# The RWKV scan of a two-block kernel: halves of heads interleaved, last tokens moved into the recurrence, chunk matrices from 32-row blocks

## What is computed

```python
def step(S, inp):
    r_t, w_t, k_t, v_t, kk_t, a_t = inp
    sa = jnp.einsum('bhvk,bhk->bhv', S, kk_t)
    S = (S * w_t[:, :, None, :]
         - sa[..., None] * (kk_t * a_t)[:, :, None, :]
         + v_t[..., None] * k_t[:, :, None, :])
    return S, jnp.einsum('bhvk,bhk->bhv', S, r_t)
```

## Time and profile before

| | us |
|---|---|
| median of 3 runs (lowest, highest) | 1706.77 (1698.46, 1707.61) |
| the profiled execution | 1702.17 |
| its span, first to last instruction | 1700.4 |
| first transpose to last addition of the scan | 567.3 to 755.2 |

### The profile page before, as it was taken

How to read it: one execution, slowest core, us unless ns; L and a number is a source line. 1 busy time by engine, 2 the same in 40 slices (tenths; PEclk the granted TensorE clock), 3 DMA queues, 4 the chain that set the end, 5 groups by cost and what they waited for, 6 DMA issues and landing times.

```text
span 1700.4 us, 32005 instructions
## 1 busy us (share of the span) xinstructions
PE 1561.2 (92%) x11384; PEld 1421.2 (84%) x11384; DVE 1072.5 (63%) x1815; ACT 838.1 (49%) x1443; POOL 411.8 (24%) x183
## 2 busy tenths in 40 slices
PE   5989879999699877778999999999999999999998
PEld 5975569999589756658899999999999988888886
DVE  3355356555666666746555989779999754555444
ACT  3445545555474311115445565667667554554554
POOL 1220102222024313001222423422221223222231
PEclk9986899999899998958999999999999999999999
DMA  6550125555134200003553555554344466566664
GB/s 225 184 161 0 50 75 185 185 185 184 64 124 149 88 1 1 2 1 124 163 164 134 187 173 183 181 158 137 130 148 138 137 195 196 186 197 190 195 194 149
DMA packets 66244, 234.80 MB, mean 138 GB/s; under 512 B 8216, under 2 KB 9256, under 8 KB 66176
## 3 DMA queue, kind: packets, MB, share of 16 engines
q1 hardware_dynamic: 65776, 232.31, 42.6%
q0 software_dynamic: 400, 1.59, 0.3%
HBM read 232.81 MB, written 1.06 MB: 138 GB/s over the span
## 4 chain that ended last, share of the span: by engine, by line
PE 72%; issue 15%; DVE 8%; ACT 2%; POOL 2%; DMA 0%; SPq 0%; POOLq 0%; DVEq 0%; ACTq 0%
PE psum L669 37%; PE psum L1154 20%; PE psum L968 4%; PE psum L683 4%; PE psum L1120 3%; DVE big L1391 2%; POOL w_lo L503 2%; PE psum L1092 1%; DVE w_lo L503 1%; PE psum L657 1%; DVE big L1503 1%; DVE big L1493 1%; DVE big L1515 0%; PE psum L1020 0%; PE psum L1017 0%
## 5 line engine op out<-in xcount | busy, mean ns | idle before, releaser
L669 PE MATMUL psum<-x_hi,w_hi 128*128 128x256 f32 (+1 forms) x2192 | 630.2, 287 | 34.8 <-DVE x_lo L1209 16.5
L503 POOL TENSOR_TENSOR w_lo<-ring,w_hi 128x1024 fp32r<-128x1024 f32 x144 | 358.0, 2486 | 1144.7 <-ACT w_hi L489 1144.7
L669 PE MATMUL psum<-x_lo,w_hi 128*128 128x256 f32 (+1 forms) x2192 | 624.8, 285 | 0.0
L669 PE MATMUL psum<-x_hi,w_lo 128*128 128x256 f32 (+1 forms) x2192 | 624.4, 285 | 0.0
L489 ACT ACTIVATE w_hi<-ring 128x1024 fp32r<-128x1024 f32 x434 | 455.9, 1051 | 111.2 <-PE psum L669 70.9
L669 PEld LDWEIGHTS psum<-x_hi,w_hi 128*128 128x128 f32 x2192 | 421.3, 192 | 42.0 <-issue 29.4
L503 DVE TENSOR_TENSOR w_lo<-ring,w_hi 128x1024 fp32r<-128x1024 f32 x290 | 364.4, 1257 | 138.0 <-ACT w_hi L489 137.2
L669 PEld LDWEIGHTS psum<-x_hi,w_lo 128*128 128x128 f32 x2192 | 421.7, 192 | 0.0
L669 PEld LDWEIGHTS psum<-x_lo,w_hi 128*128 128x128 f32 x2192 | 419.1, 191 | 0.1
L1771 DVE TENSOR_TENSOR h_lo<-big,h_hi 128x256 fp32r<-128x256 f32 x128 | 71.7, 560 | 152.9 <-ACT h_hi L2126 152.9
L1154 PE MATMUL psum<-w_hi,h_lo 128*128 128x512 f32 x512 | 157.7, 389 | 0.0
(11 more groups left out here) (293 smaller groups left out, 1773.5 us busy)
## 6 DMA issues: line engine op xcount, KB each, us to landing
ring<-experts SPq DMA_DIRECT2D x256, 512.0 KB, 3.5
ring<-w_ffn SPq DMA_DIRECT2D x66, 512.0 KB, 3.5
ring<-w_in SPq DMA_DIRECT2D x46, 512.0 KB, 3.7
ring<-w_mid SPq DMA_DIRECT2D x24, 512.0 KB, 3.5
ring<-w_out SPq DMA_DIRECT2D x16, 512.0 KB, 4.1
ring<-w_q SPq DMA_DIRECT2D x16, 512.0 KB, 4.3
ring<-w_cmp SPq DMA_DIRECT2D x8, 512.0 KB, 3.5
big<-bias_rows POOLq DMA_DIRECT2D x1, 1536.0 KB, 9.0
```

The costliest lines, as they stand in the source:

```text
L503: eng.tensor_tensor(w_lo[:, n % RING, :], ring[:, n % RING, :], w_hi[:, n % RING, :].bitcast(F32), ALU.subtract).then_inc(low_ready2 if n ...
L669: mm = pe.matmul(dst, w[:, slot, k * P:(k + 1) * P], x[:, k, t0:t0 + width], start=(n == 0), stop=(n == 3 * len(chunks) - 1))
```

## The change

- **Units.** The halves of a token group have their own `gram`, `ycol`, PSUM banks and semaphores, and run step by step in turn. `gram` has 7 slots a half instead of 10 (L4, L4T, L8T take those of L, LT, MT).
- **Last 16 tokens.** Their transposes, Grams, products and additions stand between the steps of the second group's recurrence, on PE and DVE; effects, one step and the addition remain behind it. The second group's transposes stand between the steps of the first recurrence, two a step.
- **Chunk matrices.** ACT writes kappa and beta of the turned group twice, masked by the parity of the chunk (`halves`). `carries` multiplies blocks of 32 tokens (two chunks) as 32x64 by 32x128 and 32x64 by 32x64, 80 matmuls a half, each block of rows into a bank of its own. The spreads over chunks on POOL and DVE are gone. ACT copies g after DVE's addition to f.
- **Conv pairs.** 16 pairs among the gate tiles instead of 8, the others at new places in the scan; 62 in all as before.
- The state has 3 slots instead of 9, and ACT's wait on `stay_ready` is gone.

`apply_power`, `second_products`, `third_product` and `effects` are the old matmuls with a half as argument, as are `add_power`, `add_effects` and `add_out` on DVE.

```diff
+    ("halves", 2), ("rowmask", 2), ("iota", P),
...
-tm = room(4, 4 * P)
+tm = room(2, 4 * P)
 scratch0 = at[0]
-gram = room(10, 4, P)
-ycol = room(4, P)
-f_t = room(4, 8, HD)
-g_c = room(4, 8, HD)
-state = room(4, 9, HD)
+gram = [room(7, 4, P) for _ in range(2)]
+ycol = [room(4, P) for _ in range(2)]
+f_t = room(4, 8 * HD)
+g_c = room(4, 8 * HD)
+state = room(4, 3, HD)
 top1 = at[0]
 stay = tm[:, 0, 0:14]
-
-
-expand0 = carve(8 * (T2 + 1), 2, 2, 8, HD)
-expand_g = carve(scratch0, 4, 2, 8, HD)
-expand = ((expand0[:, 0], expand0[:, 1], expand_g[:, 0]),
-          (expand_g[:, 3], expand_g[:, 2], expand_g[:, 1]))
-G_L, G_LT, G_MT, G_L2, G_L2T, G_L4, G_L4T, G_L8T, G_QT, G_RT = range(10)
+tm_kappa = carve(8 * (T2 + 1), 8, 2, HD)
+tm_beta = carve(8 * (T2 + 1) + 8 * P, 8, 2, HD)
+G_L, G_LT, G_MT, G_L2, G_L2T, G_QT, G_RT = range(7)
+G_L4, G_L4T, G_L8T = G_L, G_LT, G_MT
+FULL = {"turn": 4, "lt": (0, 4), "l": (2, 6), "qr": (0, 2), "mv": (6, 1), "l2": (4, 7), "l2t": (5, 0), "app0": (2, 3),
+        "l4": (4, 7), "l4t": (5, 0), "app1": (6, 1), "l8t": (2, 3), "app2": (4, 5), "app3": (6, 7),
+        "e": (0, 2), "o": (1, 3), "fg": (4, 0)}
+LAST = {"turn": 6, "lt": (3, 5), "l": (3, 5), "qr": (3, 5), "mv": (7, 3), "l2": (7, 3), "l2t": (7, 3), "app0": (4, 5),
+        "l4": (7, 3), "l4t": (7, 3), "app1": (6, 5), "l8t": (4, 7), "app2": (6, 5), "app3": (4, 3),
+        "e": (6, 5), "o": (7, 4)}
+banks = lambda tg: FULL if tg < 2 else LAST
+by_pair = lambda v: v.rearrange("p (r n) -> p r n", r=4)
+group = lambda tg: (tg * P, min(P, T2 - tg * P))
...
-        for hh in range(2):
-            for p in range(2):
-                u = 2 * tg + hh
-                if p == 0:
-                    pool.wait_ge(tm_ready, 4 * (tg + 1))
-                    if u > 0:
-                        pool.wait_ge(fg_sum, 2 * u - 1)
-                else:
-                    pool.wait_ge(app_ready, 4 * (u + 1))
-                for k, src in ((0, 3), (1, 1))[:2 - p]:
-                    a = (4 * hh + 2 * p) * HD
-                    pool.tensor_tensor(expand[p][k], tm[:, src, a:a + P].rearrange("p (h k) -> p h k", h=2).unsqueeze(2).to_broadcast([P, 2, 8, HD]),
-                                       const("chunk").unsqueeze(1).unsqueeze(3).to_broadcast([P, 2, 8, HD]),
-                                       ALU.mult).then_inc(spread_b, 1)
...
+    def grams(tg, hh, name, odd):
+        t0, nt = group(tg)
+        kinds = {"lt": ((beta, alpha), (kappa, alpha)), "l": ((alpha, beta),), "qr": ((beta, rho), (kappa, rho))}[name]
+        for k, (x, y) in enumerate(kinds):
+            for h in (odd, odd + 2):
+                c = gram_column(tg, name) + (2 * k + h // 2) * nt
+                mm = pe.matmul(psum[0:nt, banks(tg)[name][hh] + odd, c:c + nt], fm(x, 4 * hh + h, t0, nt),
+                               fm(y, 4 * hh + h, t0, nt), start=True, stop=True)
+        return mm
+    def product(tg, hh, name, a, rhs):
+        nt = group(tg)[1]
+        for h in range(4):
+            r = rhs(h)
+            c = column(tg, name) + h * P
+            mm = pe.matmul(psum[0:nt, banks(tg)[name][hh], c:c + r.shape[1]], gram[hh][0:nt, a, h, 0:nt], r,
+                           start=True, stop=True)
+        return mm
+    def first_products(tg, hh):
+        nt = group(tg)[1]
+        product(tg, hh, "mv", G_MT, lambda h: tm[0:nt, 1, (4 * hh + h) * HD:(4 * hh + h + 1) * HD]).then_inc(pow_sum[hh], 1)
+        product(tg, hh, "l2", G_LT, lambda h: gram[hh][0:nt, G_L, h, 0:nt]).then_inc(pow_sum[hh], 1)
+        product(tg, hh, "l2t", G_L, lambda h: gram[hh][0:nt, G_LT, h, 0:nt]).then_inc(pow_sum[hh], 1)
...
+    def carries(tg, hh):
+        b0 = FULL["fg"][hh]
+        for p in range(2):
+            for kind in range(5):
+                for x in range(2):
+                    h = 2 * p + x
+                    head = 4 * hh + h
+                    q = slice(x * HD, (x + 1) * HD)
+                    for r in range(4):
+                        rows = slice(32 * r, 32 * r + 32)
+                        c = p * P
+                        if kind == 0:
+                            mm = pe.matmul(psum[q, b0 + r, c:c + P], ycol[hh][rows, h, 0:HD],
+                                           tm_beta[rows, head].rearrange("p s k -> p (s k)"), start=True, stop=True)
+                        else:
+                            s = (kind - 1) // 2
+                            c += 2 * P + s * HD
+                            if kind % 2:
+                                mm = pe.matmul(psum[q, b0 + r, c:c + HD], tm_kappa[rows, head, s],
+                                               tm[rows, 1, head * HD:(head + 1) * HD], start=True, stop=False)
+                            else:
+                                mm = pe.matmul(psum[q, b0 + r, c:c + HD], tm_beta[rows, head, s],
+                                               ycol[hh][rows, h, HD:P], start=False, stop=True)
+        mm.then_inc(fg_sum[hh], 1)
+    def recur(tg, c):
+        n = 8 * tg + c
+        pe.wait_ge(state_ready, n + 1)
+        if tg < 2:
+            for h in range(8):
+                q = slice(h % 2 * HD, (h % 2 + 1) * HD)
+                mm = pe.matmul(psum[q, c % 2, h // 2 * HD:(h // 2 + 1) * HD], f_t[q, h // 2, c * HD:(c + 1) * HD],
+                               state[q, h // 2, n % 3, :], start=True, stop=True)
+            mm.then_inc(rec_sum, 1)
+        for h in range(8):
+            q = slice(h % 2 * HD, (h % 2 + 1) * HD)
+            mm = pe.matmul(psum[q, 2, h // 2 * P + c * CH:h // 2 * P + (c + 1) * CH], state[q, h // 2, n % 3, :],
+                           e_t[q, h // 2, c * CH:(c + 1) * CH], start=True, stop=True)
+        return mm
+    turn_in(0, range(16))
+    for tg in range(2):
         if tg > 0:
             pe.wait_ge(o_ready, tg)
         for hh in range(2):
+            if hh == 1:
+                pe.wait_ge(tm_ready, 6 * tg + 6)
             pe.wait_ge(kappa_ready, 2)
+            for name in ("lt", "l"):
                 for odd in range(2):
+                    grams(tg, hh, name, odd).then_inc(gram_sum[hh], 1)
+        for hh in range(2):
+            pe.wait_ge(gram_ready[0], 6 * tg + 2 + 2 * hh)
+            for odd in range(2):
+                grams(tg, hh, "qr", odd).then_inc(gram_sum[hh], 1)
+        pe.wait_ge(gram_ready[0], 6 * tg + 4)
+        pe.wait_ge(gram_ready[1], 6 * tg + 4)
+        first_products(tg, 0)
+        pe.wait_ge(gram_ready[0], 6 * tg + 6)
+        first_products(tg, 1)
+        pe.wait_ge(gram_ready[1], 6 * tg + 6)
+        apply_power(tg, 0, 0)
+        second_products(tg, 0)
+        apply_power(tg, 1, 0)
+        apply_power(tg, 0, 1)
+        second_products(tg, 1)
+        third_product(tg, 0)
+        apply_power(tg, 1, 1)
+        apply_power(tg, 0, 2)
+        third_product(tg, 1)
+        apply_power(tg, 1, 2)
+        apply_power(tg, 0, 3)
+        apply_power(tg, 1, 3)
+        effects(tg, 0)
+        effects(tg, 1)
+        carries(tg, 0)
+        for hh in range(2):
+            pe.wait_ge(eo_ready[hh], 2 * tg + 2)
+        carries(tg, 1)
+        for hh in range(2):
+            pe.wait_ge(f_ready[hh], 2 * tg + 2)
+            pe.wait_ge(g_ready[hh], 2 * tg + 2)
+        for c in range(8):
+            mm = recur(tg, c)
+            if c == 7:
+                mm.then_inc(out_sum, 1)
+            if tg == 0:
+                turn_in(1, (2 * c, 2 * c + 1))
+            elif c == 0:
+                turn_in(2, range(8))
+            elif c == 1:
+                for hh in range(2):
+                    if hh == 1:
+                        pe.wait_ge(tm_ready, 14)
+                    for odd in range(2):
+                        for name in ("lt", "l", "qr"):
+                            gm = grams(2, hh, name, odd)
+                        gm.then_inc(gram_sum[hh], 1)
+            elif c == 2:
+                pe.wait_ge(gram_ready[0], 18)
+                first_products(2, 0)
+                pe.wait_ge(gram_ready[1], 18)
+                first_products(2, 1)
+            elif c == 3:
+                apply_power(2, 0, 0)
+                second_products(2, 0)
+                apply_power(2, 1, 0)
+            elif c == 4:
+                apply_power(2, 0, 1)
+                second_products(2, 1)
+                third_product(2, 0)
+            elif c == 5:
+                apply_power(2, 1, 1)
+                apply_power(2, 0, 2)
+                third_product(2, 1)
+            elif c == 6:
+                apply_power(2, 1, 2)
+                apply_power(2, 0, 3)
+            elif c == 7:
+                apply_power(2, 1, 3)
+    effects(2, 0)
+    effects(2, 1)
+    for hh in range(2):
+        pe.wait_ge(eo_ready[hh], 6)
+    pe.wait_ge(o_ready, 2)
+    recur(2, 0).then_inc(out_sum, 1)
...
     for s in range(24, 32):
         low(s)
-        if s % 2:
+        conv_pair()
+        conv_pair()
...
+    for tg in range(2):
+        for hh, name in ((0, "lt"), (0, "l"), (1, "lt"), (1, "l"), (0, "qr"), (1, "qr")):
```

(81 more changed lines are left out.)

283 lines of the change are left out of this document (98 added, 185 removed).

## The result

The changed kernel takes 1673.93 us in the median of four runs (1667.35 to 1682.45), the kernel before 1706.69 beside it: ratio 0.9845, interval 0.9801 to 0.9890. A second comparison gave 1673.14 us and 0.9845 (0.9808 to 0.9881). The forecast was 1649, its range ended at 1671. The gain is 33 us where 55.5 were expected.

What follows compares the result with a forecast made beforehand. PE bounds the kernel (busy 1561.2 of 1700.4 us), each scan unit being a latency chain. Terms -16.0 + 1.4 - 23.6 - 20.5 = -58.7, with waits -55.5, gave 1646.7 to 1651.3, forecast 1649; range 1632 to 1671.

Steps and rivals of the forecast that it cites:

- Group 1: Second full token group of the scan, its two units interleaved: 40.0 us instead of 63.6, of which carries 2 x 5.0.
- Rival 1: Chunk matrices of the full groups: carries serialize wholly (+22 us) or half (+11), kernel 1660 to 1671; chance 0.17.
- rival 5: Better case in the full groups: carries at the low end, 3.3 us per half, no late DVE, kernel 1636; chance 0.12.
- Group 0: First full token group of the scan, from its first transpose: 48.2 us where u0 and u1 took 64.2.
- late masks: Start of group 0: DVE's conv pairs run into POOL's diagonal, delaying masks and first products, +3.3 us, PE idling +2.3.
- Recurrence 0: Recurrence of group 0 with group 1's transposes between its steps: 1.4 us a step, 12.5 us instead of 11.1.
- Recurrence 1 and last tokens: Second recurrence with the last 16 tokens between its steps: 28.5 us instead of 49.0.
- 15 us at full clock: PE work of the last 16 tokens in recurrence 1: 27.24 us at granted clock 0.56, taken as 15 at full clock.
- Rival 2: Recurrence 1: last group isn't hidden and the clock falls to half; with tail about 41 us, kernel 1661; chance 0.15.
- After the scan nothing changes but PE's clock (0 to 2 us): Code behind the scan: claimed unchanged except for PE's clock, 0 to 2 us.
- Waits: Whole scan: some 30 handovers of 0.1 us each that the sum leaves out, turning -58.7 into -55.5.
- Rivals 3 and 4: Scan: TensorE stays at its lower level, 1757 us, chance 0.03; interleaved units wait for each other, 1677 us, chance 0.06.

Runs made afterwards that it cites:

- e5: Changed kernel with 8 of 16 conv pairs moved from the gate tiles to recurrence 1 (six) and behind the scan (two): 1664.10 us, ratio 0.9802.
- e1: Changed kernel plus three f32 filler matmuls, read by nobody, in PE's gap after the carries of each full group: 1662.84 us, ratio 0.9796.
- e2: Changed kernel with group 1's 16 transposes put into the gap after group 0's carries, none between recurrence 0's steps: 1664.42 us, ratio 0.9811.
- e11: Kernel before with its constant table 10 columns wider, giving tensors behind it the changed kernel's addresses modulo 64 bytes: 1708.00 us against 1703.30, ratio 1.0042.
- e9: Changed kernel with e6's table, e5's conv pairs, e2's transposes, and the last tokens' transposes plus two fillers ahead of recurrence 1: 1640.96 us, ratio 0.9645.
- e10: e9 with the last 16 tokens' products reading whole 128x128 weight blocks instead of 16-row ones: 1656.22 us, ratio 0.9715.
- e8: e1 plus a 256-column filler matmul, read by nobody, behind each of steps 2 to 7 of recurrence 1: 1665.78 us, ratio 0.9805.
- e6: Changed kernel with the `halves` constant widened from 2 to 8 columns, so SBUF tensors behind it keep their old addresses: 1654.59 us, ratio 0.9741.

## Why the prediction was off, point by point

- **Group 1, 40.0 forecast, 39.4 measured.** The interleaving is costed about rightly, and PE fills its product stage (18.7 us from the Grams to the effects, forecast 17.4). But two terms were wrong and cancelled. The Grams took 8.5 us instead of 6.3, since the half clock of recurrence 0 lasted until 634.8. The carries took 5.9 us for both halves instead of 10.0: in group 0 the first half took 1.9 us for 160 records, 599.83 to 601.75, 12 ns each, below the low end of 3.3:

```profile
599.83 0.47 PE L1005 MATMUL psum<-big 32*64 32x128 f32 x16
...
601.76 0.47 PE L1005 MATMUL psum<-big 32*64 32x128 f32 x14
```

 Cheaper carries alone could not bring the end of a group forward by as much: in group 0 DVE works without a pause from 591.66 to 607.53 on additions, effects and conv pairs, and its last addition to f is the last thing in that stretch. Behind it stands the gap. The forecast's own sum had PE idle there, 2.9 us for the last additions and the copies of g; 3.19 were measured. The idle time was foreseen, what it does to the clock was not asked. Rival 1 (carries serialize) falls; rival 5's cheap carries came, its gain didn't. The Trainium skill (TensorE: Matmul & The Clock Gate, LDWEIGHTS) has a weight load take its columns over 1.2 GHz; an estimate from that figure, 8.5 us a half in series, is far off here. The Trainium skill (TensorEngine Tiling (Array Packing), Key Properties) also has different tiles load and multiply in parallel, and the 12 ns agree with that.
- **Group 0, 48.2 forecast, 47.2 measured.** The forecast counts 1.3 us of a later start that the measured stage can't hold; without it the two are 46.9 and 47.2. The late masks were foreseen, but the row behind them was misread. The 3.97 us of the earlier trace rows are not beside POOL's diagonal, which had ended at 572.26, but beside its two spreads of 128x1024, one conv instruction beside each (the lines under e5). In the changed kernel the spreads are gone and one conv instruction took 3.92 us beside the diagonal, one 2.60 beside the split ahead of it. That the size came out is in part luck. Moving the conv pairs (e5) gave 7.8 us, where the forecast had 3.3 + 2.3 = 5.6 for them within the stage.
- **Recurrence 0, 12.5 forecast, 20.2 measured.** The step of 1.4 us assumed 1.00 of the clock, because both recurrences of the earlier trace rows had it. The step that failed is that inference. The changed kernel has a gap of 3.19 us ahead of the recurrence where the kernel before had one of 2.55 and, 6 us later, one of 0.78, and behind it every step ran at 0.50, 2.4 us each. With the gap filled e1 and e2 give 12.5 and 11.2 us. Nor was the 1.00 safe before: e11, with the old schedule, lost it in the third step.
- **Recurrence 1 and last tokens, 28.5 forecast, 41.2 measured.** "15 us at full clock" is the term that failed. Rival 2, with a chance of 0.15, named the fall of the clock and the price (41, 1661 us in all). That the price came out to the microsecond is luck: its mechanism, the clock falling with the small records, makes 36.8 to 37.0 us where the recurrence starts at 1.00 (e1, e9), and the other 4.2 us came from a start at half clock behind the gap, which the rival doesn't name. The lower clock of 0.56 in the earlier trace rows can't be put down to the waits between these records: it also falls with PE 97 to 100% busy (e1, e9) and stays down. What in them lets it fall stays open. More rows of the array in the products don't bring it back (e10), and some dense filler among them doesn't hold it (e8).
- **"After the scan nothing changes but PE's clock (0 to 2 us)"** was wrong by 10.6 us. The diff shows the 8-column entry turn into 2 columns, and I read it as a change of a mask. Taken off the measured 1673.9 it leaves 1663.3, inside the range; e6, with the old addresses, measured 1654.6.
- **Waits**, 3.2 us for what a sum leaves out: groups 0 and 1 came out 1.6 us under the sum, 1.3 of it the later start named above, so in the groups they weren't needed. Rivals 3 and 4 did not come.

The sum again, with what was measured: 7.7 + 12.7 from the clock, 10.6 from the addresses, −1.6 from the groups, −3.2 for the waits allowed, make 26.2; less 5.6 us of the shorter start of that profile 20.6, which is what the profiled span shows (1665.6 + 1.8 against 1646.7).

## What to carry to other kernels

Where a forecast's sum has PE idle, ask what clock the matmuls behind it will get: here some 3 us of idle time, foreseen and priced at 3 us, stood ahead of a recurrence that then ran at half clock for 20 us; put work that is due anyway into such a gap. Cost a stretch of matmuls at the granted clock that the same records had before, not at full clock, until a run shows what lowered it. And where they had full clock in one profile, look at a second one before relying on it. And a diff that alters the width of a constant table moves every tensor behind it: compare the length of untouched matmuls ahead of and behind the change.
